# Expert weights in twelve 1 MB ring slots (8 KB runs) instead of six of 2 MB (16 KB runs)

## What is computed

```
proj = x @ w_in                                  # q, k, v, u
a = stick_breaking_attention(q, k, v);  s = GLU(S5_SSM(u))
h = LN1(alpha*x + [rms(a)*g_attn | rms(s)*g_ssm] @ w_out)
group = top1(softmax(h @ w_rg + b_rg));  e1, e2 = top2 of the group's 8 experts
moe = sum over e1, e2 of gate_e * ((silu(h @ w_gate[e]) * (h @ w_up[e])) @ w_down[e])
y = LN2(alpha*h + moe + sigmoid(h @ w_ple_gate) * (p @ w_ple_proj))
```

## Time and profile before

| | us |
|---|---|
| median of 3 runs (1729.96 to 1732.61) | 1731.1 |
| profiled execution, device time | 1734.78 |
| its span, first to last instruction | 1733.1 |
| PE busy in it | 1506.7 |
| DVE busy in it | 569.4 |
| DMA, mean over the span | 300 GB/s |
| granted TensorE clock, mean | 0.959 |

### The profile page before, as it was taken

The page is one execution under the profiler, slowest core; times in us unless marked ns, Lnnn a source line. Parts: engine busy times, 40 slices in busy tenths (PEclk is TensorE's granted clock), DMA queues, the critical chain, the costliest instruction groups (busy, mean ns, idle before and its releaser), DMA issues.

```text
span 1733.1 us, 22921 instructions
## 1 busy us (share of the span) xinstructions
PE 1506.7 (87%) x8820; PEld 971.0 (56%) x8820; DVE 569.4 (33%) x1019; ACT 139.7 (8%) x294; POOL 228.0 (13%) x366
## 2 busy tenths in 40 slices
PE   4999999999999869989879879889879698877775
PEld 2777777777777746545545545545535355534433
DVE  6988888874110421111102101011210111111114
ACT  3011111113000300000000000000000000000001
POOL 2666666600000010000000000000000000000003
PEclk9999999999999789999999999999999999999997
DMA  7554454533586159999999999999999999999964
GB/s 177 132 142 121 125 138 116 140 105 87 156 291 220 33 207 387 406 416 410 416 415 402 416 413 409 404 414 411 399 400 414 403 404 414 417 410 414 418 238 166
DMA packets 175370, 520.06 MB, mean 300 GB/s; under 512 B 23536, under 2 KB 135280, under 8 KB 148016
## 3 DMA queue, kind: packets, MB, share of 16 engines
q1 hardware_dynamic: 160032, 485.73, 73.1%
q10 hardware_dynamic: 13120, 17.90, 3.2%
q0 software_dynamic: 2128, 15.21, 3.1%
HBM read 496.85 MB, written 21.95 MB: 299 GB/s over the span
## 4 chain that ended last, share of the span: by engine, by line
PE 43%; DMA 42%; DVE 8%; issue 3%; SPq 1%; ACT 1%; POOL 1%; ACTq 0%; POOLq 0%; DVEq 0%
DMA e_ring<-in_w_exp_up_dram 37%; PE bank L988 14%; PE bank L1324 11%; DMA e_ring<-in_w_exp_gate_dram 4%; PE bank L1343 3%; PE bank L1278 3%; PE bank L1208 2%; PE bank L1138 2%; DVE e_ring L1508 1%; PE bank L1022 1%; SPq L573 1%; PE bank L1030 1%; DMA rows_by_expert<-rows,idx 1%; PE bank L1249 1%; PE bank L999 1%
## 5 line engine op out<-in xcount | busy, mean ns | idle before, releaser
L1324 PE MATMUL bank<-e_ring,xT_exp 128*64 128x256 f32 x4096 | 478.0, 391 | 109.2 <-DMA e_ring<-in_w_exp_gate_dram 63.3
L1324 PEld LDWEIGHTS bank<-e_ring,xT_exp 128*64 128x64 f32 x4096 | 295.0, 141 | 302.6 <-DMA e_ring<-in_w_exp_gate_dram 84.8
L1343 PE MATMUL bank<-e_ring,hidT 128*64 128x512 f32 x1024 | 247.9, 641 | 42.2 <-DVE hidT L1826 42.2
L988 PE MATMUL bank<-xT,w_ring 128*128 128x288 f32 x1024 | 259.0, 412 | 0.7 <-issue 0.7
L988 PEld LDWEIGHTS bank<-xT,w_ring 128*128 128x128 f32 x1024 | 193.8, 192 | 57.2 <-issue 5.1
L1821 DVE TENSOR_TENSOR hid<-bank,sig_exp 128x256 f32<-128x256 f32 x32 | 13.6, 425 | 570.9 <-ACT sig_exp L942 570.9
L1343 PEld LDWEIGHTS bank<-e_ring,hidT 128*64 128x64 f32 x1024 | 75.5, 147 | 192.5 <-issue 143.5
L741 POOL DMA_INDIRECT e_ring<-expert_rows_out,idx x6 | 5.6, 928 | 1077.6 <-ACT all_stored_mark L751 1076.1
L1278 PE MATMUL bank<-hT,w_ring 128*128 128x288 f32 (+2 forms) x640 | 134.9, 370 | 0.0
L1278 PEld LDWEIGHTS bank<-hT,w_ring 128*128 128x128 f32 x640 | 110.7, 191 | 18.9
L1832 DVE COPY rows<-bank 128x512 f32<-128x512 f32 x32 | 22.1, 692 | 242.6 <-PE bank L1343 242.6
(11 more groups left out here) (303 smaller groups left out, 1160.8 us busy)
## 6 DMA issues: line engine op xcount, KB each, us to landing
e_ring<-in_w_exp_gate_dram SPq DMA_DIRECT2D x64, 2048.0 KB, 27.0
e_ring<-in_w_exp_up_dram SPq DMA_DIRECT2D x64, 2048.0 KB, 28.1
e_ring<-in_w_exp_down_dram SPq DMA_DIRECT2D x64, 2048.0 KB, 23.1
w_ring<-in_w_in_dram SPq DMA_DIRECT2D x32, 1024.0 KB, 6.4
w_ring<-in_w_out_dram SPq DMA_DIRECT2D x16, 1024.0 KB, 6.8
w_ring<-in_w_ple_gate_dram SPq DMA_DIRECT2D x16, 1024.0 KB, 23.9
expert_rows_out<-hT POOLq DMA_DIRECT2D x3, 1536.0 KB, 9.5
w_ring<-in_ssm_w_glu_dram SPq DMA_DIRECT2D x4, 1024.0 KB, 5.2
```

Of the source, the lines that this page charges most:

```text
L988: last_mm = pe.matmul(out, weights(k), moving[:, k, :], start=(k == 0), stop=(k == n - 1))
L1324: mm = pe.matmul(gu[h * B:(h + 1) * B, s % 2, :], xT_exp[:, c, s // 2, :], w[:, c, h * FH:(h + 1) * FH], start=(s == 0 and c == 0), stop=( ...
L1343: mm = pe.matmul(bank[h * B:(h + 1) * B, 3 + n, :], hidT[:, c, half, :], e_ring[:, 2 * (NGU + half) + c, h * DH2 + n * 512:h * DH2 + (n + ...
```

## The change

`NEW` goes from 6 to 12 and `NGU`, the number of gate and up slots, from 4 to 8. The ring keeps its 12 x 8 KB per partition. A piece is now 4 matrix rows per partition of gate or up (8 KB contiguous, out of the 16 KB that the partition takes from this half), or one row of down. The order is gate 0a, up 0a, gate 0b, up 0b, gate 1a, up 1a, gate 1b, up 1b, then down 0a, 0b, 1a, 1b. TensorE runs the same matmuls in the same accumulation, with a wait and an `ew_used` increment per 1 MB slot; the order among gate and up changes with the order of the pieces. In the down product the loops go by slot. With expert 0, two 1 MB pieces follow each odd `w_out` slice.

```diff
--- before.py
+++ after.py
@@ -145,9 +145,9 @@
         hT = sb("hT", [P, KC, T])
         mergedT = hT
         w_ring = sb("w_ring", [P, 4, D])
-        NEW = 6
-        NGU = 4
-        e_ring = sb("e_ring", [P, 2 * NEW, D])
+        NEW = 12
+        NGU = 8
+        e_ring = sb("e_ring", [P, NEW, D])
         rows = sb("rows", [P, NT, D])
         DH2, FH = D // 2, FE // 2
 
@@ -563,13 +563,14 @@
                 if not first:
                     sp.wait_ge(ew_used, b * NEW + (s + 1 - NEW))
                     settled()
-                piece = e_ring[:, 2 * s:2 * s + 2, :]
+                piece = e_ring[:, s:s + 1, :]
                 if s < NGU:
-                    src = (wg_v, wu_v)[s % 2][:, ds(e, 1), s // 2, :, :]
-                    dst = piece.rearrange("p (a b) n -> p a (b n)", a=1).rearrange("p a (k f) -> p a k f", f=FE)
+                    q = s // 2 % 2 * 4
+                    src = (wg_v, wu_v)[s % 2][:, ds(e, 1), s // 4, q:q + 4, :]
+                    dst = piece.rearrange("p a (k f) -> p a k f", f=FE)
                 else:
-                    src = wd_v[:, ds(e, 1), s - NGU, :, :]
-                    dst = piece.rearrange("p (a b) n -> p a b n", a=1)
+                    src = wd_v[:, ds(e, 1), (s - NGU) // 2, s % 2, :]
+                    dst = piece
                 sp.dma_start(dst, src).then_inc(ew_landed[s], 16)
 
             def expert_load(b, e):
@@ -583,7 +584,8 @@
             for m in range(4, KC):
                 w_load(m % 4, N_OUT + m - 3, w_out_v[:, :, m * P:(m + 1) * P])
                 if m % 2:
-                    expert_piece(0, 0, (m - 4) // 2, True)
+                    expert_piece(0, 0, m - 5, True)
+                    expert_piece(0, 0, m - 4, True)
 
             def ple_gate_load(n, j, slot, wait):
 
@@ -1317,12 +1319,12 @@
                 gu = bank[:, 0, :].rearrange("p (g n) -> p g n", g=2)
                 for s in range(NGU):
                     pe.wait_ge(ew_landed[s], b * 16 + 16)
-                    w = e_ring[:, 2 * s:2 * s + 2, :].rearrange("p b (k f) -> p (b k) f", f=FE)
-                    for c in range(RUN):
+                    w = e_ring[:, s, :].rearrange("p (k f) -> p k f", f=FE)
+                    for c in range(4):
                         for h in range(2):
 
-                            mm = pe.matmul(gu[h * B:(h + 1) * B, s % 2, :], xT_exp[:, c, s // 2, :], w[:, c, h * FH:(h + 1) * FH],
-                                           start=(s == 0 and c == 0), stop=(s >= 2 and c == RUN - 1), skip_group_check=True)
+                            mm = pe.matmul(gu[h * B:(h + 1) * B, s % 2, :], xT_exp[:, s // 2 % 2 * 4 + c, s // 4, :], w[:, c, h * FH:(h + 1) * FH],
+                                           start=(s == 0 and c == 0), stop=(s >= NGU - 2 and c == 3), skip_group_check=True)
                     mm.then_inc(ew_used, 1)
                 x_turn(b + 1)
                 if middle is not None:
@@ -1335,14 +1337,13 @@
                 if not first:
                     pe.wait_ge(ye_act, b)
                     pe.wait_ge(ye_dve, b)
-                for half in range(2):
-                    pe.wait_ge(ew_landed[NGU + half], b * 16 + 16)
-                    for c in range(2):
-                        for n in range(2):
-                            for h in range(2):
-                                mm = pe.matmul(bank[h * B:(h + 1) * B, 3 + n, :], hidT[:, c, half, :],
-                                               e_ring[:, 2 * (NGU + half) + c, h * DH2 + n * 512:h * DH2 + (n + 1) * 512],
-                                               start=(half == 0 and c == 0), stop=(half == 1 and c == 1))
+                for s in range(NGU, NEW):
+                    pe.wait_ge(ew_landed[s], b * 16 + 16)
+                    for n in range(2):
+                        for h in range(2):
+                            mm = pe.matmul(bank[h * B:(h + 1) * B, 3 + n, :], hidT[:, s % 2, (s - NGU) // 2, :],
+                                           e_ring[:, s, h * DH2 + n * 512:h * DH2 + (n + 1) * 512],
+                                           start=(s == NGU), stop=(s == NEW - 1))
                     mm.then_inc(ew_used, 1)
 
             def pair(n, j):
```

## The result

| | before | after |
|---|---|---|
| median of 6 runs, us | 1731.94 | 1737.43 |
| range | 1729.96 to 1733.24 | 1734.47 to 1738.63 |
| profiled execution, us | 1734.78 | 1737.62 |
| its span | 1733.1 | 1736.0 |

The ratio is 1.0034, 95% interval [1.0024, 1.0044]: slower by 5.5 us, where 6.8 had been forecast. The two profiled executions lie only 2.8 us apart.

A forecast was written before the change was run, and what follows sets the result against it. The prediction took the DMA engines, never idle at 410 GB/s while 31 experts are fetched, as the bound. Packets +10.4, beginning -1.8 and end -1.8 made +6.8 us on 1731.1: 1737.9 us, range 1725 to 1747.

The forecast's parts named there:

- What bounds the kernel: In the stage of 31 experts, DMA engines never idle at 410 GB/s while TensorE keeps up; engine time per byte decides.
- The price of packets: Full expert stage: 8 KB instead of 16 KB packets cost 7 ns more for every 16 KB, 10.4 us.
- the lower end: Smallest packet cost for the stage, from 619.4 against 615.7 ns in the full stage: 3.7 ns, 5.5 us.
- The beginning, -1.8: Stage start: the next load is issued after the first quarter of expert 0's down matmuls instead of half, saving 1.8 us.
- The end, -1.8: Stage end: only 16 instead of 32 TensorE instructions remain after the last up landing, saving 1.8 us.
- The sum: Whole kernel: +10.4 - 1.8 - 1.8 = +6.8 us, 1737.9 us as the median.
- Costed at nothing: SP's doubled issues, holds from the queue's depth, six more TensorE waits an expert, expert 0's load among w_out: no cost.
- A: Full stage: packets cost only 5.5 us, the two ends give 3.6 back: +1.9, 1733.0 us; 27%.
- B: Rate dips once an expert, 0.9 us each: smaller packets halve them, 14 us back, -7.2 us, 1723.9; 14%.
- C: Full stage: extra packets cost nothing, only the two ends change: -3.6 us, 1727.5; 10%.
- D: Full stage: half-runs cost 13 ns per extra packet, +15.7, 1746.8 us, or memory dislikes the new order; 7%.
- The fixed cost per transfer: Expert loads: about 2 us for each of 186 more transfers, 372 us if one after another; left 1%.

The follow-up runs named there:

- packets-alone run: Kernel before with its six slots and 2 MB transfers, each partition's two 8 KB halves put apart in the ring, giving 8 KB packets: 1740.1 us beside 1733.0.

## Why the prediction was right

*What bounds the kernel*: right. The stage's rate decided, and the engines never ran dry by the traces.

*The price of packets*: right in kind; its size came out near the truth by two errors against each other. 10.4 us were forecast and the packets-alone run shows 7.1. But where q1 is alone an extra packet costs about 10 ns by bytes over wall time, not 7: 14 us over the stage. Against that, some 6 us of 880, 7 over the stage, came back beside other transfers, the row loads above all, a term that the sum had at nothing. "Nothing ties the dip to the size of q1's packets" was the step that failed: the same six slots with 16, 8 and 4 KB packets lost 39, 31 and 23 us. The windows that the price was read from were good to some 2 ns, 612 and 619 where longer stretches show 611 and 621. The saturated row, 616, held packets of q10 as well, and the lower end taken from it, 5.5 us, was no price of a packet. The forecast of 619 to 623 ns per 16 KB for the stage was wrong by its base as well: over 740 to 1640 us q1's records, dips included, were at 640 before (96.9% of 14400 us for 357.10 MB) and are at 650 after.

*The beginning, -1.8*: 1.72 by the trace (3.69 to 1.97). SP's first issue came 3.7 us after TensorE's start instead of the 2.7 forecast (5.2 before), which changed nothing there. *The end, -1.8*: 1.73 (7.80 to 6.07). Taken alone and timed, both gave 2.1 us, interval 1.0 to 4.2, less than the 3.5 of the traces but not at odds with it.

*The sum*: 14 for packets, about 7 back beside other transfers, at most 1.5 for reports, 3.5 back at the ends would be 4 to 5; measured 5.5 and 5.8, and 3.7 with contiguous pieces. The forecast of 6.8 came close since a price some 4 us too low stood beside a gain of some 7 us that was left out. The direction and the two ends were reasoned, the closeness was in part luck.

*Costed at nothing*: SP's doubled issues and the holds in the queue cost nothing that shows. The holds became the rule, as forecast, with a DMA share of 1.02. The waits on TensorE and the load of expert 0 don't show either. What did count was the loss beside the row loads.

*Rivals*: A, too little to see, had a figure nearer to the net price and the wrong verdict, though its 1733.0 is not far below the lowest runs of after. B had its mechanism right at about half its size, some 0.2 us an expert, near the 0.22 from which it was said to decide; it lost to a packet price higher than the one it was set against. C fell by the packets-alone run. D's 13 ns per packet was above the 10 that the stretches with q1 alone show.

The fixed cost per transfer that the Trainium skill names (DMA: Bandwidth & Descriptors, Anatomy of one DMA), and names for transfers that GpSimd issues, doesn't show in SP's queue here: 186 more transfers come to at most 1.5 us. The overhead per packet in the Trainium skill (DMA: Bandwidth & Descriptors, Why small descriptors are slow), by which I had estimated 3.5 ns a packet, is a third of the 10 ns measured with q1 alone; the measurement decides.

## What to carry to other kernels

In a stage that the DMA engines bound, a finer ring gains only at the two ends, and there the first and last pieces can be cut finer alone; cutting all of them pays for each packet, here about 10 ns per packet and engine between 16 and 4 KB, of which a half (8 KB) or a third (4 KB) came back beside other transfers. Price packets by bytes over wall time in stretches where one queue is alone, and what is lost beside others by itself: a sum over the whole stage hides both. Then look at who else uses the engines: small transfers to few partitions slowed the whole stream here, and sending twice the bytes to all 128 partitions was worth 21 us.

## What was not expected of the hardware

- Transfers to 64 neighbouring partitions at a time, alternating between the halves, moved 228 GB/s instead of 410, with 1160 ns per 16 KB packet instead of 640.
- Row loads of 64 to 256 KB per transfer, two per expert, cost about 33 us beyond their bytes in a kernel of 1732 us; as one transfer to 128 partitions with 0.5 MB they left no dip, at 425 GB/s.
- Smaller packets in the large stream made those row loads disturb it less: 39, 31 and 23 us lost of 880 with 16, 8 and 4 KB packets, while each extra packet cost 10 ns where the stream was alone.
- With twelve 1 MB pieces of 9 descriptors per engine outstanding, SP is held in an issue for about 2 us, and four issues take 10.36. ACT's issues aren't held meanwhile: its row load goes out 1.1 us into one such hold and its store 6.3 us into another.

```profile
943.11 2.10 SPq L574 DMA_DIRECT2D e_ring<-in_w_exp_up_dram  x1
...
944.21 0.86 ACTq L929 DMA_DIRECT2D rows<-rows_by_expert  x2
...
957.10 0.86 ACTq L939 DMA_DIRECT2D expert_rows_out<-rows  x2
```

It is not the number of pieces: with six pieces an issue took over 1 us 6 times in 175 with 16 KB packets, 44 in 175 with 8 KB and 145 in 172 with 4 KB. That the number of descriptors outstanding is what holds SP fits this, but no run varied it alone.
